# Six row layouts for one activation buffer in a two-block transformer kernel

## The reference

```python
h = h + mix @ w_out
u = rms_norm(h, mlp_norm_g)
h = h + jnp.square(jax.nn.relu(u @ w_up)) @ w_down
...
for i in range(DEPTH_2):          # i = 0: MLA, i = 1: sliding window
    h = rmsnorm(x, layer_norm[i])
    ...
    x = x + (y * jax.nn.silu(gate)) @ w_out
return rmsnorm(x, final_norm)
```

## The kernel before

| buffer | begins at byte | bytes from row to row | read by |
|---|---|---|---|
| `u` | 65664 | 2176, the two halves 1088 apart (512 columns are then two runs) | projections of the first block |
| `ux` (over `u`) | 65664 | 2144 | `up0` to `up3`, `mla_in`, MLA gates, `swa_kv`, `swa` |
| `ya` | 100480 | 2144 | `merge`, `down0` to `down3`, `mla_out`, `swa_out` |
| `yb` | 134784 | 2048 | `merge` |
| `mx` | 167552 | 2048 | `out` |
| `w_hi`, `w_lo` | 32896, 49280 | 512 from block to block | every product |

## Time and profile before

### The profile page before, as it was taken

One profiled execution on the slowest core, in us unless ns is written; L12 is line 12 of the kernel. 1 busy time (PEld: TensorE's weight loads), 2 busy tenths in 40 slices (PEclk: granted clock), 3 DMA queues, 4 the chain that ended last, 5 costly groups with the idle time before them and its releaser, 6 DMA issues.

```text
span 2748.1 us, 50879 instructions
## 1 busy us (share of the span) xinstructions
PE 2717.4 (99%) x17597; PEld 2457.1 (89%) x17597; DVE 2032.3 (74%) x3698; ACT 1417.0 (52%) x2469; POOL 310.3 (11%) x323
## 2 busy tenths in 40 slices
PE   7999999999999999999999999999999999999998
PEld 7999999999998888888888888888888998888887
DVE  7888888888888566567765666656777767788875
ACT  6566566656655434334443544534545455455553
POOL 0000000000000000004700000000460002400024
PEclk9999999999999999999999999999999999999999
DMA  6444444444444555556566555655555544544445
GB/s 226 147 155 146 156 149 151 156 139 160 148 151 144 177 189 187 189 189 215 177 194 192 184 193 181 194 190 182 195 183 177 164 166 159 188 164 142 146 154 183
DMA packets 130236, 472.74 MB, mean 172 GB/s; under 512 B 15136, under 2 KB 15136, under 8 KB 129952
## 3 DMA queue, kind: packets, MB, share of 16 engines
q1 hardware_dynamic: 126144, 457.37, 51.1%
q0 software_dynamic: 3936, 13.34, 1.6%
HBM read 468.40 MB, written 2.25 MB: 171 GB/s over the span
## 4 chain that ended last, share of the span: by engine, by line
PE 96%; DVE 2%; ACT 1%; issue 1%; DMA 0%; DVEq 0%; SPq 0%; ACTq 0%
PE bank L318 41%; PE bank L319 21%; PE bank L320 8%; PE bank L322 8%; PE bank L321 7%; PE bank L902 1%; PE bank L857 1%; PE bank L911 1%; DVE w_lo L294 1%; PE bank L1126 1%; PE bank L1286 1%; PE bank L969 0%; PE bank L1203 0%; ACT w_hi L288 0%; PE bank L1302 0%
## 5 line engine op out<-in xcount | busy, mean ns | idle before, releaser
L294 DVE TENSOR_TENSOR w_lo<-raw,w_hi 128x1024 fp32r<-128x1024 f32 x862 | 1058.7, 1253 | 159.1 <-ACT w_hi L288 156.5
L288 ACT ACTIVATE w_hi<-raw 128x1024 fp32r<-128x1024 f32 x862 | 896.2, 1052 | 430.1 <-PE bank L319 424.0
L318 PE MATMUL bank<-ya,w_hi 128*128 128x512 f32 x1792 | 625.3, 393 | 0.7 <-DVE h L2273 0.7
L318 PE MATMUL bank<-ux,w_hi 128*128 128x512 f32 x1744 | 621.1, 398 | 0.1
L319 PE MATMUL bank<-ya,w_lo 128*128 128x256 f32 x1792 | 500.9, 279 | 0.0
L319 PE MATMUL bank<-ux,w_lo 128*128 128x256 f32 x1744 | 487.6, 280 | 0.0
L320 PE MATMUL bank<-u,w_hi 128*128 128x272 f32 (+1 forms) x1296 | 408.3, 315 | 4.8 <-DVE u L445 2.9
L318 PEld LDWEIGHTS bank<-ya,w_hi 128*128 128x128 f32 x1792 | 336.6, 188 | 77.3 <-issue 2.2
L318 PEld LDWEIGHTS bank<-ux,w_hi 128*128 128x128 f32 x1744 | 327.6, 188 | 74.1 <-issue 2.9
L322 PE MATMUL bank<-u,w_lo 128*128 128x272 f32 (+1 forms) x1296 | 373.2, 288 | 0.0
L321 PE MATMUL bank<-u,w_hi 128*128 128x272 f32 (+1 forms) x1296 | 372.8, 288 | 0.0
(11 more groups left out here) (422 smaller groups left out, 3831.0 us busy)
## 6 DMA issues: line engine op xcount, KB each, us to landing
raw<-in_stream SPq DMA_DIRECT2D x864, 512.0 KB, 3.4
mix_row<-rows POOLq DMA_DIRECT2D x16, 408.0 KB, 4.9
xT<-in_xT SPq DMA_DIRECT2D x4, 544.0 KB, 5.6
mix_coef_m<-meta_rows POOLq DMA_DIRECT2D x16, 128.0 KB, 3.4
h<-in_xT POOLq DMA_DIRECT2D x1, 2048.0 KB, 9.7
out_dram<-h SPq DMA_DIRECT2D x8, 256.0 KB, 2.4
consts<-in_consts POOLq DMA_DIRECT2D x1, 1817.0 KB, 11.7
meta_rows<-mix_b_mat POOLq DMA_DIRECT2D x16, 1.0 KB, 3.6
```

Of the source, the lines that this page charges most:

```text
L288: act.activation(w_hi[:, slot], raw[:, slot], ACT.Copy).then_inc(hi_ready, 1)
L294: dve.tensor_tensor(w_lo[:, slot], raw[:, slot], w_hi[:, slot].bitcast(F32), ALU.subtract).then_inc(lo_ready, 1)
L318: pe.matmul(o, a, x, start=first, stop=False)
```

## The change

Each of the six stages that read `ya` after `merge` gets a view of the region of its own. A view is a tensor placed over the same bytes with its own distance from row to row; only the first 512 floats of a row are used. The sum of used bytes and the work are the same. `merge` keeps the old view, and the four `up` stages keep rows of 2144 bytes in `ux`.

```diff
+        def rows_of(name, where, row, gap):
+            both = place(name, [P, KT, row], F32R, where)[:, :, 0:2 * (SEQ + gap)]
+            return both.rearrange("p k (a n) -> p k a n", a=2)[:, :, :, 0:SEQ]
+
+        ROWS = {"down0": rows_of("rows_down0", ya_at + 64, 2 * SEQ, 0),
+                "down1": rows_of("rows_down1", ya_at, 2 * SEQ + 8, 0),
+                "down2": rows_of("rows_down2", ya_at, 2 * SEQ + 4, 0),
+                "down3": rows_of("rows_down3", ya_at, 2 * SEQ + 20, 0),
+                "mla_out": rows_of("rows_mla", ya_at, 2 * SEQ + 16, 0),
+                "swa_out": rows_of("rows_swa", ya_at - 384, 2 * SEQ + 32, 0)}
...
-                matrix(f"down{q}", ya, ("hidden lo", (q + 1) * KT, 1))
+                matrix(f"down{q}", rows_for(f"down{q}"), ("hidden lo", (q + 1) * KT, 1))
...
-            matrix("mla_out", ya, ("mla lo", HEADS // 2, 2), begun=True)
+            matrix("mla_out", rows_for("mla_out"), ("mla lo", HEADS // 2, 2), begun=True)
...
-            matrix("swa_out", ya, ("swa lo", KT, 1), begun=True)
+            matrix("swa_out", rows_for("swa_out"), ("swa lo", KT, 1), begun=True)
...
-                act.activation(ya_x[:, k, 0, :], sum_t[:, s, None, :], ACT.Copy).then_inc(sem("hidden hi"), 1)
+                act.activation(ROWS[f"down{q}"][:, k, 0, :], sum_t[:, s, None, :], ACT.Copy).then_inc(sem("hidden hi"), 1)
...
-                dve.tensor_tensor(ya_x[:, t, 1, :], sum_t[:, s, None, :], ya_x[:, t, 0, :].bitcast(F32),
+                o = ROWS[f"down{q}"]
+                dve.tensor_tensor(o[:, t, 1, :], sum_t[:, s, None, :], o[:, t, 0, :].bitcast(F32),
```

More of the change, by code:

```diff
@@ L360, in ya, with rows_for, x @@
             return ya_x[:, k]
+        def rows_for(stage):
+            def x(k):
+                return ROWS[stage][:, k]
+            return x
         def yb(k):
@@ L1226, in _ @@
             for w in range(windows(MLA_UNIT, PAIRS, MLA_PE)):
-                stream_ = mla_products(w) if w < PAIRS else first_blocks("mla_out", ya, ("mla lo", PAIRS - 1))
+                stream_ = mla_products(w) if w < PAIRS else first_blocks("mla_out", rows_for("mla_out"), ("mla lo", PAIRS - 1))
                 steps = window(MLA_PE, w, MLA_UNIT, PAIRS) if w < PAIRS else [(at, w, step) for at, *step in MLA_PE_END]
@@ L1308, in _ @@
                         "out": swa_out}
-            out_left = first_blocks("swa_out", ya, ("swa lo", BEGUN_BLOCKS))
+            out_left = first_blocks("swa_out", rows_for("swa_out"), ("swa lo", BEGUN_BLOCKS))
             for w in range(windows(SWA_UNIT, KT, SWA_PE)):
@@ L1744, in mla_y_hi @@
                 act.wait_ge(sem("mla y"), n)
-                act.activation(ya_x[:, 2 * n - 2:2 * n, 0, :], y_v[:], ACT.Copy).then_inc(sem("mla hi"), 1)
+                act.activation(ROWS["mla_out"][:, 2 * n - 2:2 * n, 0, :], y_v[:], ACT.Copy).then_inc(sem("mla hi"), 1)
             steps_act = {"evac": mla_evac, "evac qr": mla_evac_qr, "tanh": mla_tanh,
@@ L1796, in swa_y_hi @@
                 act.wait_ge(sem("swa y"), n)
-                act.activation(ya_x[:, bass.ts(n - 1, 1), 0, :], s_y[:, None, :], ACT.Copy).then_inc(
+                act.activation(ROWS["swa_out"][:, bass.ts(n - 1, 1), 0, :], s_y[:, None, :], ACT.Copy).then_inc(
                     sem("swa hi"), 1)
@@ L2428, in mla_y_lo @@
                 t = slice(2 * n - 2, 2 * n)
-                dve.tensor_tensor(ya_x[:, t, 1, :], y_v[:], ya_x[:, t, 0, :].bitcast(F32),
+                o = ROWS["mla_out"]
+                dve.tensor_tensor(o[:, t, 1, :], y_v[:], o[:, t, 0, :].bitcast(F32),
                                   ALU.subtract).then_inc(sem("mla lo"), 1)
@@ L2507, in swa_y_lo @@
                 t = bass.ts(n - 1, 1)
-                dve.tensor_tensor(ya_x[:, t, 1, :], s_y[:, None, :], ya_x[:, t, 0, :].bitcast(F32),
+                o = ROWS["swa_out"]
+                dve.tensor_tensor(o[:, t, 1, :], s_y[:, None, :], o[:, t, 0, :].bitcast(F32),
                                   ALU.subtract).then_inc(sem("swa lo"), 1)
```

## The result

The changed kernel takes 2754.8 us, median of 19 runs (2753.16 to 2756.9), against 2750.75 us for the kernel before, also of 19, on the same chips (one of these took 5441.36 us, which a median does not feel). The ratio is 1.0015, 95% interval 1.0009 to 1.0021: slower by 0.15%, under the 0.2% that I called no change. The forecast was 2751.3 us.

The account below looks back on a forecast made before the run. TensorE's matmul pairs were taken to bound the kernel. Stage terms of -0.4, 0, 0, 0, +0.1, +0.7 us gave +0.4, plus a 0.6 us lean: span 2749.1 us, with 2.25 us to the median 2751.3 us; range 2745.5 to 2758.

Parts of the forecast that it names:

- TensorE's matmuls bound the stages, one ns on a pair is one on the time: All six stages: TensorE busy 88.90 of 88.90 us in `down0`; only the time of a matmul pair, 347.5 ns, counts.
- the rule of the read ports: TensorE's matmuls: two independent read ports, so every layout would cost the same and the sum be 0.
- Rival 1: All six stages: no effect at all, something other than the offset separates `out` from `down0`; 2750.35 us, chance 0.07.
- Each offset has its own price, to be added up: First matmul of a pair: each row offset costs its own time, 8 ns between best (64) and worst (0).
- The steps of 16 and 80, put at 0 each: `down2` (rows 2064) and `down3` (2128): sixteen offsets, eight unpriced, taken at mean 392.1 ns; 0 us each.
- `swa_out`, put at +0.7 as two slow offsets: `swa_out`, rows 2176: offsets 128 and 0, mean 395.0 ns, 2.9 ns more, +0.7 us.
- `down0` at -0.4 us: `down0`, offset 64 always: 388 + 2.7 ns for repetition, 1.4 ns under 392.1; 256 pairs give -0.4 us.
- The sum: All six stages: terms of +0.4 us and a lean of 0.6 us, +1.0 us on the span.
- the lean of 0.6 us: All six stages: 0.4 ns a pair added upward, as 2144 is the quickest of three layouts in the trace.
- Rival 2: Repetition and neighbours decide: `down0`, `mla_out`, `swa_out` at 353.6 ns, others 2 to 6 ns slower; 2758 us, chance 0.14.
- The signs that it named: New profile: wrong if stage deviations share a sign and reach 4 ns; `down1` 347 to 348, `down0` median 388 to 391.
- The bounds taken from the rows of the trace: First matmul's duration: 387 ns, least of any `down0` row, and 403, most in a layout with one offset.

Follow-up runs that it names:

- wshift: Kernel before with `w_hi` and `w_lo` begun 64 bytes later, activations at the same place modulo 256; 2748.16 us, timed once.
- wstep: Kernel before with weight blocks 536 instead of 512 bytes apart and rows of 2048 bytes in all stages reading `ya`; 2764.17 us, timed once.
- map1: Changed kernel with `down` rows 2064 apart read in steps 48, 112, 144, 176 and `up` rows in 96, 32, 224, 160; 2757.05 us, timed once.
- map2: As map1, but `down0` to `down3` rows 2080, 2080, 2112, 2064 apart, read in steps 96, 160, 192, 240; 2753.98 us, timed once.
- const: Changed kernel with rows of 2048 bytes in all six stages, at constant offsets 0, 32, 64, 128, 192, 96; 2756.17 us, timed once.
- fast64: `w_lo` 64 bytes later, `ya`, `yb`, `ux`, `mx` rows 2048 apart at offset 64 against `w_hi`; 2742.55 us, ratio 0.9965 to the kernel before.
- fast64x: As fast64, but only `ya` at offset 64, `ux`, `mx`, `yb` at 0; median 2734.05 us, ratio 0.9939 to the kernel before.
- map32: `w_lo` 32 bytes later; constant offsets 0, 32, 64, 96, 128, 160 in the six stages, 224 in `up`; 2752.59 us, timed once.
- map128: `w_lo` 128 bytes later; constant offsets 0, 64, 128, 192, 32, 96 in the six stages, 160 in `up`; 2753.28 us, timed once.
- five: Changed kernel with `down0` back at rows of 2144 bytes; median 2754.89 us, ratio 1.0013 to the kernel before.

## Why the prediction was right, and where not

*TensorE's matmuls bound the stages, one ns on a pair is one on the time.* Right: 4.4 us of pairs, 4.05 us between medians, no new wait.

*The layout has an effect, against the rule of the read ports.* Right. Rival 1 falls: the steps alone move a stage between 347.5 and 352.2 ns. By the Trainium skill (SBUF — State Buffer, "Who interferes with whom") TensorE's two read ports are independent and it never waits on anyone; these runs do not agree, and the measurement decides: the same pairs took from 340.0 to 353.3 ns. wshift and the `up` stages of wstep show that a stage's time hangs on where the moving rows stand against the weights being loaded. Whether they meet in the memory or elsewhere no run shows.

*Each offset has its own price, to be added up.* This step failed. `down1`, "the same eight offsets in another order: 0 us", took +0.85 us, and in map1 and map2 stages with the same eight offsets took 347.5, 350.0 or 350.8 ns. The durations in the earlier trace rows belonged to the order of the rows there, not to each offset alone. The steps of 16 and 80, put at 0 each, took +1.19 and +0.33; `mla_out`, put at +0.1, +0.40; `swa_out`, put at +0.7 as two slow offsets, only +0.16: named as the slowest of the six, it was the quickest, 348.3 ns a pair.

*`down0` at -0.4 us.* Mis-sized with the wrong sign: +1.48. The 388 ns of the one row at offset 64 did not survive repetition; the stage runs at 353.3, the value of `out`. I had priced repetition at 2.7 ns from offset 0 alone. By const and fast64 a constant layout has no one price.

*The sum.* +1.0 us forecast, +4.4 measured in the stages: the lean of 0.6 us towards "2144 is the best of three" was the right thought at a seventh of its size. Rival 2 was nearer to the mechanism, neighbours before offsets, with a size of 6.2 to 9.3 us that was too large: it put `mla_out` and `swa_out` at 353.6 ns, and they took 349.1 and 348.3. Its picture, that few offsets and close ones are slow, does not hold as a rule either: `down1` of const, with a single offset, took 346.7.

*The signs that it named.* The one for being wrong came: all six deviations are upward and two pass 4 ns, `down0` with +5.8 and `down2` with +4.7. `down1` was not at 347 to 348, and the median of `down0`, 397, is the sign of rival 2 and not of the best offset. The time fell into the range all the same. As far as the prices of the offsets go, that is luck; the range itself came from the rows of two measured layouts, and the six stages lay between these.

*The range and the writers.* The bounds taken from the rows of the trace, 387 and 403 ns of duration, held all six stages. They hold for these layouts only: fast64x runs at 340.0 ns a pair, under the 342.4 that 387 stood for. The writer of the high parts keeps its time:

```profile
L1660 ACT ACTIVATE rows_down<-mlp_sum x64: 417/417/420, 1335.1 to 1956.9; 128x256 f32 x62, 128x256 fp32r<-128x256 f32 x2
```

## What to carry to other kernels

Where pairs of a weight load and a matmul follow each other without a gap, look at how the moving operand's address moves against the weights' from one to the next: here it is worth up to 1.7% of a stage between one step and another, and up to 3.9% (340.0 against 353.3 ns) between constant offsets, and the order of the sum is a free way to choose it. A duration read inside a repeating pattern belongs to the pattern; do not carry it to another one as the price of an address. And where a profile shows whole stages, compare stage by stage before comparing spans: one stretch of half clock was worth a third of this change.

## What the runs showed of the hardware

- Time of a 512-column and a 256-column fp32r matmul with their weight loads, by the step of the offset modulo 256: 353.3 (0), 352.2 (16), 350.8 (32), 349.1 (64), 348.8 (80), 347.5 (96), 348.3 (128), 350.0 (160, 192, 224) ns. Other steps are off any smooth curve through these (48 351.3, 112 351.1). With a step the value repeated to 0.1 ns between the executions compared.
- With no step the pair settles at a value between 340.0 and 353.3 ns, often 340.0, 346.7, 350.0 or 353.3, and keeps it over hundreds of pairs; inside a stage it changed only behind a slow start. Four layouts were each seen at two values: `out` at 346.7 and 353.3, fast64 at 340.0 and 350.0, the `up` stages of map32 at 348.4 and 351.1 and those of map128 at 346.7 and 350.0. What decides between the two stays open.
- The clock went to its lower level for a stretch after a 1.9 us wait of TensorE at the same place, in seven of 14 profiled executions; the wait itself was in all 14. The timed runs of `five` and of the kernel before had a mean clock of 0.999 or of 0.998, those with 0.998 some 1.5 us longer.
